# Expert units of one head by 128 tokens in place of four heads by 32 tokens

## The chip, the cores and the metric

The kernel runs on one core of one Trainium2 chip. The metric is the device time of one execution in microseconds (us). The kernel before took 1830.41 us (median of three runs, 1829.29 to 1832.8). All arrays are float32.

## What is computed

Two blocks follow one another on 256 tokens of width 1024. The first (four mixers and a dense MLP) is untouched by the change. The second has 16 more tokens in front ("meta"), and two layers, each of which ends in PEER, a lookup of experts:

```python
q = einsum('btd,dq->btq', hx, w_query)            # 8 heads x 2 halves x 128
s = einsum('bthpc,hpnc->bthpn', q, sub_keys)      # 128 scores in each half
top_s, top_i = top_k(s, 16)
cand = top_s[..., 0, :, None] + top_s[..., 1, None, :]
best_s, best_pos = top_k(cand, 16)                # 16 experts per token and head
gate = softmax(best_s)
act = gelu(einsum('btd,bthkd->bthk', hx, u[expert]))
y = einsum('bthk,bthkd->btd', gate * act, v[expert])
```

So each of 256 tokens takes 8 x 16 = 128 pairs of rows u and v in each of two layers. A pair stands as 2048 numbers (8 KB) in one table in HBM. Between the two PEER layers stands one attention layer (products with w_kv, w_q, w_o, a loop over eight pairs of heads, then the query product of the second PEER).

## The kernel before, in words

The PEER work of both layers is one long pipeline of 512 *slots*. A slot is one gather of 128 rows of the table (1 MB, one row for each partition). 16 slots make a *unit* and 32 units follow one another: 8 for each of layer 0 tile 0, layer 0 tile 1, layer 1 tile 0, layer 1 tile 1, a tile being 128 tokens. The text counts in steps x of four slots: step x holds slots 4x to 4x+3 and unit x//4.

Before the change a unit is (layer, tile, g, half): the 32 tokens of group g, with four heads side by side in the four quarters of the partitions. Two units (half 0 and 1) finish a group.

A slot passes through these places:
- GpSimd issues the gather (peer_gpsimd, L634) into one of eight buffers (RING = 8), once the slot eight before it has been used up (v_used).
- VectorE multiplies the u half of the row by the token's own row and sums it (dots_of, L675). The tokens' rows stand in PSUM banks 2 and 3 (rows_x); unit_rows (L647) puts them there anew for every group, after the last dot of the group before. dots_of waits for it (rows_ready).
- ScalarE makes a 128x32 matrix: gelu(dot) times a selection matrix (L706), then times the gate (L710). The selection matrix sel32 has a one where partition p belongs to token p mod 32.
- TensorE multiplies this matrix by the v half of the row, in two halves of 512 columns (slot_value, L662). The output has 32 partitions. Even slots write partitions 0 to 63 of the bank, odd slots 64 to 127, so that the four quarters of the array are used in turn; two banks alternate from group to group.
- After a group VectorE adds four pieces of 32x512 to the residual h (add_group, L722).

In each step TensorE executes, in the written order (peer_tensor, L775): late_queries_pe (steps 0 to 15: L384 scores, L366 transposes of the queries, L349 the query product of a later unit), then for each of the four slots pieces of the attention (attend_pe) and the slot's own product. ATTEND = (34, 66) is the step at which the attention of tile 0 and of tile 1 begins; from there count steps i. Products with weights (product, L824; L828 for the meta tokens, tile 0 only) stand in i = 2, 3 (query), 4, 5 (key), 6, 7 (value), and later for w_o and the second query product: four in a step, two before its first slot and two before its second. The loop over the pairs of heads starts at i = 9 (tile 0) or 8 (tile 1). The weights come through six buffers of 512 KB from SP's queue. VectorE's and ScalarE's orders are written out by hand in the same steps. The routing of units (top-16 searches) is spread over the steps by the tables EARLY and LATE.

At the end (s = 31) zero_products keeps TensorE busy between slots, the last group is added, and each group of 32 rows is stored on its own (L1660).

## Time and profile before

| | us |
|---|---|
| median of three runs | 1830.41 |
| lowest, highest | 1829.29, 1832.8 |
| span of the profiled execution, first to last instruction | 1826.5 |
| TensorE busy | 1366.8 |
| VectorE busy | 1169.7 |
| ScalarE busy | 597.3 |
| GpSimd busy | 551.0 |

The time of a run contains some us before the first and after the last instruction: 1830.4 less 1826.5 is 3.9 us. The PEER pipeline begins at about 388 us with the first gather and ends with the span. "Busy" of TensorE counts matmuls that overlap once. "PEclk" is the share of the full clock (2.4 GHz) that TensorE was granted: 1.0 is 2.4 GHz, 0.5 is 1.2 GHz, a value between is a mean over both.

### The profile page before, as it was taken

What the parts mean: (1) busy time and instruction counts of PE and PEld (TensorE: products, weight loads), DVE (VectorE), ACT (ScalarE), POOL (GpSimd) and SP (SyncE); (2) the same over time, 40 slices, a digit from 0 to 9 for tenths busy, and PEclk for the clock granted to TensorE, in tenths of its full rate; (3) what the DMA queues carried; (4) which work ended last, traced back from release to release, by engine and by line L of the source; (5) the groups of instructions that cost most, each with busy time, mean ns of one, the idle gap of its engine ahead of it and who ended that gap; (6) DMA issues with size and microseconds to landing.
All of it is one profiled execution on the core that took longest, in us unless ns stands there. A gap on an engine that the chain in (4) does not pass through costs nothing.

```text
span 1826.5 us, 21618 instructions
## 1 busy us (share of the span) xinstructions
PE 1366.8 (75%) x7080; PEld 550.5 (30%) x7080; DVE 1169.7 (64%) x2705; ACT 597.3 (33%) x1530; POOL 551.0 (30%) x633
## 2 busy tenths in 40 slices
PE   8999999988874545698678865776787765655566
PEld 7856666653430010122122221221232210101011
DVE  5831334277776777656786647767877577677764
ACT  2421011124342323433443323433443333333332
POOL 2001232023332333322433224322342333333331
PEclk9999999999996676799777878897898977666677
DMA  9048697559999999999999999999999999999997
GB/s 358 5 176 345 204 373 263 230 211 419 420 420 419 417 415 417 420 417 409 417 392 418 416 418 406 419 417 416 384 410 418 420 421 421 421 422 418 418 421 292
DMA packets 118194, 681.29 MB, mean 373 GB/s; under 512 B 11790, under 2 KB 13970, under 8 KB 50114
## 3 DMA queue, kind: packets, MB, share of 16 engines
q0 software_dynamic: 78336, 553.68, 73.6%
q1 hardware_dynamic: 39745, 126.23, 18.0%
q8 instruction: 56, 0.92, 0.2%
q14 instruction: 57, 0.46, 0.1%
HBM read 678.30 MB, written 1.05 MB: 372 GB/s over the span
## 4 chain that ended last, share of the span: by engine, by line
DMA 37%; PE 29%; DVE 13%; ACT 4%; issue 3%; DVEq 3%; POOL 2%; ACTq 1%; POOLq 0%
DMA big<-in_peer_uv,expert 33%; PE ps L662 7%; DVE big L675 6%; PE ps L1900 6%; PE ps L1889 6%; PE ps L824 5%; DMA normed<-in_peer_uv,expert 5%; DVEq L528 2%; POOL big L634 2%; PE ps L647 2%; DVE residual L722 1%; ACT placed L706 1%; ACT L706 1%; ACT placed L710 1%; ACT L683 1%
## 5 line engine op out<-in xcount | busy, mean ns | idle before, releaser
L662 PE MATMUL ps<-big,placed 128*32 128x512 f32 x1992 | 596.1, 795 | 393.9 <-ACT placed L710 391.8
L675 DVE CUSTOM_DVE_ANT_0 big<-big,ps 128x1024 f32<-128x1024 f32 x498 | 595.7, 1219 | 340.4 <-DMA big<-in_peer_uv,expert 322.9
L634 POOL DMA_INDIRECT big<-in_peer_uv,expert x498 | 473.8, 951 | 1016.7 <-PE ps L662 855.9
L706 ACT ACTIVATE placed<-sel,dots 128x32 f32<-128x32 f32 x512 | 163.5, 319 | 797.2 <-DVE dots L675 789.6
L662 PEld LDWEIGHTS ps<-big,placed 128*32 128x32 f32 x1992 | 80.8, 122 | 820.5 <-ACT placed L710 734.7
L824 PE MATMUL ps<-big 128*128 128x512 f32 x384 | 187.2, 624 | 2.5 <-DVE big L1129 1.4
L710 ACT ACTIVATE placed<-placed,gate 128x32 f32<-128x32 f32 x512 | 164.6, 321 | 35.4 <-issue 0.3
L1900 PE MATMUL ps<-big,sc 128*128 128x512 f32 x256 | 115.5, 595 | 0.0
L1889 PE MATMUL ps<-ua,big 128*128 128x256 f32 (+1 forms) x512 | 110.4, 370 | 2.9 <-PEq L75 2.9
L824 PEld LDWEIGHTS ps<-big 128*128 128x128 f32 x384 | 69.8, 196 | 116.6 <-issue 108.7
L1889 PEld LDWEIGHTS ps<-ua,big 128*128 128x128 f32 x512 | 94.1, 194 | 27.8 <-issue 17.7
L1725 ACT ACTIVATE sc<-ps 128x256 f32<-128x256 f32 (+1 forms) x32 | 11.8, 370 | 173.2 <-PE ps L1889 173.2
L1517 PE MATMUL ps<-sc,big 128*128 128x256 f32 x288 | 63.6, 379 | 1.9 <-DMA big<-in_w_in 1.6
L349 PE MATMUL ps<-big 128*32 128x256 f32 x1024 | 61.5, 394 | 3.6 <-DVE big L278 3.6
L1900 PEld LDWEIGHTS ps<-big,sc 128*128 128x128 f32 x256 | 48.0, 190 | 49.5 <-issue 48.1
L1517 PEld LDWEIGHTS ps<-sc,big 128*128 128x128 f32 x288 | 54.0, 189 | 11.0 <-DVE sc L1367 2.1
L611 POOL DMA_INDIRECT big<-in_peer_uv,expert x32 | 38.9, 1216 | 60.4 <-DVE expert L572 26.6
L706 ACT ACT_TABLE_LOAD x40 | 51.3, 1283 | 1.1 <-issue 0.5
L722 DVE TENSOR_TENSOR residual<-residual,ps 32x512 f32<-32x512 f32 x64 | 43.7, 684 | 2.4 <-PE ps L662 0.5
L647 PE MATMUL ps<-ident,big 128*32 128x128 f32 x960 | 43.6, 326 | 0.4 <-DVE dots L675 0.4
L675 DVE DVE_READ_ACCUMULATOR2_ANT dots<- 128x1 f32 x512 | 42.2, 82 | 0.0
L647 PEld LDWEIGHTS ps<-ident,big 128*32 128x32 f32 x960 | 36.1, 130 | 18.1 <-issue 10.3
(371 smaller groups left out, 1280.2 us busy)
## 6 DMA issues: line engine op xcount, KB each, us to landing
big<-in_mlp_w SPq DMA_DIRECT2D x16, 2048.0 KB, 15.9
big<-in_peer_wq SPq DMA_DIRECT2D x2, 8192.0 KB, 26.9
big<-in_w_kv SPq DMA_DIRECT2D x32, 512.0 KB, 14.2
big<-in_peer_wq SPq DMA_DIRECT2D x32, 512.0 KB, 13.2
big<-in_w_in SPq DMA_DIRECT2D x5, 2048.0 KB, 17.8
big<-in_peer_uv,expert POOLq DMA_INDIRECT x530, 15.0
big<-in_w_q SPq DMA_DIRECT2D x16, 512.0 KB, 14.0
big<-in_w_o SPq DMA_DIRECT2D x16, 512.0 KB, 10.3
```

What stands on the lines that cost most here:

```text
L349: last = nc.tensor.matmul(bank(4 + u % 2)[TOK * j:TOK * (j + 1), 0:256], hnt[:, k, at:at + TOK], wq_peer[:, k, cols:cols + 256], start=(k ...
L634: nc.gpsimd.indirect_dma_start(out=pair_row(n), out_offset=None, in_=rows, in_offset=bass.IndirectOffsetOnAxis(ap=expert[:, n // TOPK % DE ...
L647: last = nc.tensor.matmul(to[TOK * j:TOK * (j + 1), :], hnt[:, k, at:at + TOK], ident[:], start=True, stop=True)
L662: last = nc.tensor.matmul(acc[r:r + TOK, :], placed[:, n % RING, :], pair_row(n)[:, D + BANK * half:D + BANK * (half + 1)], start=(opens a ...
L675: nc.vector.tensor_tensor_reduce(out=row, in0=row, in1=rows_x, scale=1.0, scalar=0.0, op0=ALU.mult, op1=ALU.add, accum_out=dots[:, u % 2, ...
L706: a.activation(to, sel32[:], ACT.Gelu, scale=dots[:, u % 2, k:k + 1])
L710: a.activation(to, to, ACT.Copy, scale=gate[:, u % DEEP, k:k + 1]).then_inc(S(f"weights_ready{UNITS[u][0]}"), 1)
L722: last = v.tensor_tensor(to, to, bank(group % 2)[r:r + TOK, :], ALU.add)
L824: last = m.matmul(bank(b + half), src, w[:, BANK * half:BANK * (half + 1)], start=(k == 0), stop=(k == KD - 1))
L1517: last = m.matmul(bank(b)[:, T * c:T * (c + 1)], win[chunk][:, k, P * (at + c):P * (at + c + 1)], ht[:, k, :], start=(k == 0), stop=(k == ...
L1889: last = m.matmul(bank(4 + q % UP_BANKS)[:, first:T], w1b[c % 2][:, k, P * (q % FT):P * (q % FT + 1)], h2t[:, k, first:T], start=(k == 0), ...
L1900: last = m.matmul(bank(2 * t + half), act2[:, q % FT, P * t:P * (t + 1)], w2b[c % 2][:, q % FT, BANK * half:BANK * (half + 1)], start=(q = ...
```

## The change

A unit becomes (layer, tile, head): all 128 tokens of a tile and one head, one token for each partition.
- The matrix of a slot becomes 128x128 with the weights on the diagonal (gelu times the identity), and slot_value multiplies it over the whole width of the array. All 128 slots of a tile add up in banks 0 and 1.
- The four adds per group become two adds of 128x512 per tile (add_tile). They stand after the second dot of the next tile; the first product of the next tile waits for both.
- unit_rows runs once per tile and transposes eight 128x128 blocks.
- The query product, the scores and the second PEER's scores become 128 wide.
- The output is stored in halves of 512 columns for each tile.
- The matrix select, its four copies on GpSimd, and sel32 go.

```diff
-        placed = sb("placed", [P, RING, 32])
-        sel32 = sb("sel32", [P, 32])
+        placed = sb("placed", [P, RING, P])
@@ tile_units
-            return [(layer, t, g, half) for g in range(QUADS) for half in range(2)]
+            return [(layer, t, head) for head in range(PH)]
@@ queries_pe
-                for j in range(QUADS):
-                    cols = D * half + 256 * j
-                    last = nc.tensor.matmul(bank(4 + u % 2)[TOK * j:TOK * (j + 1), 0:256], hnt[:, k, at:at + TOK],
-                                            wq_peer[:, k, cols:cols + 256], start=(k == 0), stop=(k == KD - 1))
+                last = nc.tensor.matmul(bank(4 + u % 2)[:, 0:256], hnt[:, k, at:at + P],
+                                        wq_peer[:, k, 256 * head:256 * (head + 1)], start=(k == 0), stop=(k == KD - 1))
@@ scores0_pe
-            for j in range(QUADS):
-                for p in range(2):
-                    last = nc.tensor.matmul(bank(7)[TOK * j:TOK * (j + 1), P * p:P * (p + 1)],
-                                            q_cols[u % 2][:, P * p + TOK * j:P * p + TOK * (j + 1)],
-                                            keys_t0[:, 2 * (QUADS * half + j) + p, :], start=True, stop=True)
+            for p in range(2):
+                last = nc.tensor.matmul(bank(7)[:, P * p:P * (p + 1)], q_cols[u % 2][:, P * p:P * (p + 1)],
+                                        keys_t0[:, 2 * head + p, :], start=True, stop=True)
@@ unit_rows
-            slots_done(pe, "dots_done", TOPK * u)
+            if u:
+                slots_done(pe, "dots_done", TOPK * u)
             for k in range(KD):
-                to = bank(2 + k // 4)[:, P * (k % 4):P * (k % 4 + 1)]
-                for j in range(QUADS):
-                    last = nc.tensor.matmul(to[TOK * j:TOK * (j + 1), :], hnt[:, k, at:at + TOK], ident[:],
-                                            start=True, stop=True)
+                last = nc.tensor.transpose(bank(2 + k // 4)[:, P * (k % 4):P * (k % 4 + 1)], hnt[:, k, at:at + P], ident[:])
@@ slot_value
-            if k == 0 and opens and group >= 2:
-                pe.wait_ge(S("tile_out"), group - 1)
+            if first and u:
+                sums_out(pe, u // PH)
             slots_done(pe, "weights_ready", n + 1)
             for half in range(2):
-                r = 2 * TOK * (k % 2) + TOK * half
-                last = nc.tensor.matmul(acc[r:r + TOK, :], placed[:, n % RING, :],
-                                        pair_row(n)[:, D + BANK * half:D + BANK * (half + 1)],
-                                        start=(opens and k < 2), stop=(closes and k >= TOPK - 2))
+                last = nc.tensor.matmul(bank(half), placed[:, n % RING, :],
+                                        pair_row(n)[:, D + BANK * half:D + BANK * (half + 1)], start=first, stop=final)
@@ slot_weight
-            a.activation(to, sel32[:], ACT.Gelu, scale=dots[:, u % 2, k:k + 1])
+            a.activation(to, ident[:], ACT.Gelu, scale=dots[:, u % 2, k:k + 1])
@@ add_group becomes add_tile
-            for par in range(2):
-                slots_done(dve, "v_used", TOPK * (u + 1) - 1 + par)
-                for half in range(2):
-                    r = 2 * TOK * par + TOK * half
-                    to = h[TOK * g:TOK * (g + 1), t, BANK * half:BANK * (half + 1)]
-                    last = v.tensor_tensor(to, to, bank(group % 2)[r:r + TOK, :], ALU.add)
-                dve.drain()
-            last.then_inc(S("tile_out"), 1)
+            slots_done(dve, "v_used", TOPK * (u + 1))
+            for half in range(2):
+                to = h[:, t, BANK * half:BANK * (half + 1)]
+                step(dve, nc.vector.tensor_tensor(to, to, bank(half), ALU.add), "tile_out")
@@ peer_vector
-                    ahead = j == 0 and s > 0 and opens_group(s)
+                    ahead = j == 0 and s > 0 and opens_tile(s)
                     if ahead:
                         routes_at(dve, s, j)
-                    dots_of(dve, s, range(4 * j, 4 * j + 4))
-                    if j == 1 and s >= 1 and closes_group(s - 1):
-                        add_group(dve, s - 1)
-                    if not ahead:
+                        dots_of(dve, s, range(0, 2))
+                        add_tile(dve, s - 1)
+                        dots_of(dve, s, range(2, 4))
+                    else:
+                        dots_of(dve, s, range(4 * j, 4 * j + 4))
                         routes_at(dve, s, j)
@@ attend_pe (scores of the second PEER)
-                for g in range(QUADS):
+                for j in range(QUADS):
                     for p in range(2):
-                        for j in range(QUADS):
-                            hp = 2 * (QUADS * half + j) + p
-                            last = m.matmul(bank(6 + g // 2)[TOK * j:TOK * (j + 1), 256 * (g % 2) + P * p:256 * (g % 2) + P * (p + 1)],
-                                            qt1[:, hp, TOK * g:TOK * (g + 1)], keys_t1[:, hp, :], start=True, stop=True)
+                        hp = 2 * (QUADS * half + j) + p
+                        at = 256 * (j % 2) + P * p
+                        last = m.matmul(bank(6 + j // 2)[:, at:at + P], qt1[:, hp, :], keys_t1[:, hp, :], start=True, stop=True)
@@ the stores
-                    for g in range(QUADS):
-                        r = slice(TOK * g, TOK * (g + 1))
-                        sp.wait_ge(S("tile_out"), QUADS * (NT + t) + g + 1)
-                        sp.dma_start(out_v[r, t, :], h[r, t, :]).then_inc(S("out_stored"), 16)
+                    for half in range(2):
+                        cols = slice(BANK * half, BANK * (half + 1))
+                        sp.wait_ge(S("tile_out"), 2 * (NT + t) + half + 1)
+                        sp.dma_start(out_v[:, t, cols], h[:, t, cols]).then_inc(S("out_stored"), 16)
```

## Rows read from the trace of the kernel before

**Rows 1.** The page, part 2: the span in 40 slices of 45.7 us

```profile
DMA  9048697559999999999999999999999999999997
GB/s 358 5 176 345 204 373 263 230 211 419 420 420 419 417 415 417 420 417 409 417 392 418 416 418 406 419 417 416 384 410 418 420 421 421 421 422 418 418 421 292
```

**Rows 2.** Windows: us, busy of PE, PEld, DVE, ACT, POOL, PEclk, DMA share, GB/s

```profile
399.00:539.00 140.00, 117.74 (x1414) 52.84 (x1408) 111.18 (x289) 56.06 (x166) 51.71 (x55) 0.94 1.01 420
774.00:869.00 95.00, 84.25 (x339) 26.76 (x341) 55.58 (x122) 32.17 (x74) 22.47 (x24) 0.95 1.01 414
1510.00:1800.00 290.00, 171.32 (x652) 28.23 (x652) 204.17 (x469) 93.29 (x256) 107.80 (x115) 0.68 1.01 420
```

**Rows 3.** Windows: two stretches at borders of groups, same columns

```profile
927.00:944.00 17.00, 15.76 (x134) 6.46 (x134) 13.14 (x27) 7.90 (x27) 7.64 (x8) 0.91 0.93 338
1312.00:1332.00 20.00, 19.10 (x142) 8.43 (x140) 14.78 (x27) 9.22 (x27) 8.19 (x8) 0.82 0.87 324
```

**Rows 4.** Timeline, VectorE at the border before unit 20: start, us, what, [idle before]

```profile
1320.62 1.22 DVE L675 CUSTOM_DVE_ANT_0 big<-big,ps 128x1024 f32<-128x1024 f32 x1 [4.67 <-PE ps L647]
```

**Rows 5.** Groups with forms: busy, mean ns of one, idle before

```profile
L722 DVE TENSOR_TENSOR residual<-residual,ps 32x512 f32<-32x512 f32 x64 | 43.7, 684 | 2.4 <-PE ps L662 0.5
L706 ACT ACTIVATE placed<-sel,dots 128x32 f32<-128x32 f32 x512 | 163.5, 319 | 797.2 <-DVE dots L675 789.6 <-PE ps L662 6.8
L1730 ACT ACTIVATE sc<-sc 128x256 f32<-128x256 f32 x32 | 13.3, 416 | 2.6
```

**Rows 6.** Timeline, TensorE, a query product and the slots behind it

```profile
449.15 3.66 PE L349 MATMUL ps<-big 128*32 128x256 f32 x64
452.63 1.04 PE L662 MATMUL ps<-big,placed 128*32 128x512 f32 x8
```

**Rows 7.** Timeline, TensorE, around the head of the pipeline

```profile
383.18 3.72 PE L1993 MATMUL ps<-big 128*128 128x256 f32 x16
398.69 6.52 PE L349 MATMUL ps<-big 128*32 128x256 f32 x64 [3.58 <-DVE big L278]
```

**Rows 8.** Timeline, TensorE, products and slots of the attention of tile 0

```profile
782.69 3.70 PE L824 MATMUL ps<-big 128*128 128x512 f32 x8
786.35 1.05 PE L662 MATMUL ps<-big,placed 128*32 128x512 f32 x4
787.33 3.70 PE L824 MATMUL ps<-big 128*128 128x512 f32 x8
...
831.66 3.26 PE L647 MATMUL ps<-ident,big 128*32 128x128 f32 x58
...
836.10 1.88 PE L824 MATMUL ps<-big 128*128 128x512 f32 x4
837.92 1.05 PE L828 MATMUL ps<-big 128*32 128x512 f32 x4
838.90 1.99 PE L824 MATMUL ps<-big 128*128 128x512 f32 x4
...
849.32 1.98 PE L824 MATMUL ps<-big 128*128 128x512 f32 x4
```

**Rows 9.** The chain that ended last, gathers in it: issue, us to landing

```profile
529.84 15.34 DMA big<-in_peer_uv,expert
868.76 12.60 DMA big<-in_peer_uv,expert
```

**Rows 10.** Gathers issued from 1312 to 1332 (tile big, GpSimd)

```profile
DMA to landing us min/median/max: 7.4/8.7/10.6
```

**Rows 11.** Timeline, the last slot and the end

```profile
1819.89 1.04 PE L261 MATMUL ps<-zeros 128*128 128x512 bf16 x4
...
1821.38 1.05 PE L662 MATMUL ps<-big,placed 128*32 128x512 f32 x4 [0.45 <-ACT placed L710]
1822.47 1.40 DVE L722 TENSOR_TENSOR residual<-residual,ps 32x512 f32<-32x512 f32 x2 [0.48 <-PE ps L662]
```

**Rows 12.** Timeline, TensorE waiting in the loop over pairs of heads

```profile
1338.05 0.28 PE L905 MATMUL ps<-ident,big 128*16 128x128 f32 x1 [2.82 <-DVE big L1206]
```

More of the change, by code:

```diff
@@ L376, in scores0_pe @@
         def scores0_pe(pe, u):
-            half = UNITS[u][3]
+            head = UNITS[u][2]
             pe.wait_ge(S("q_out"), u + 1)
@@ L407, in peer_head_pe @@
             pe.wait_ge(S("h1"), 4)
-            for half in range(2):
-                last = nc.tensor.matmul(bank(2 + half), select[:], ffn0_rows[:, BANK * half:BANK * (half + 1)],
-                                        start=True, stop=True)
-            last.then_inc(S("rows_ready"), 1)
+            unit_rows(pe, 0)
             query_columns_pe(pe, 1)
@@ L1692, in _ @@
                 step(pool, g.memset(half_col[:], 0.5), "masks_ready")
-                for j in range(QUADS):
-                    step(pool, g.tensor_copy(select[:, TOK * j:TOK * (j + 1)], ident[:, 0:TOK]), "masks_ready")
                 pool.wait_ge(S("meta_q_done"), 1)
```

60 lines of the change are left out of this document (25 added, 35 removed).

## The prediction

> **What bounds the kernel now.** I read the page's slices first: from slice 9 (411 us) to the end the DMA engines are busy for 9 tenths or more, and move 410 to 422 GB/s in nearly every slice [rows 1]. A gather is 128 x 8192 bytes = 1.049 MB, so at 420 GB/s a slot costs 2.50 us and a step of four slots 9.99 us, whoever works on it. Then the windows: in the plain stretch 1510 to 1800 TensorE is busy 171 of 290 us at a mean clock of 0.68, VectorE 204 of 290, ScalarE 93 of 290 [rows 2]. None of them sets the pace there. In the first steps (399 to 539) TensorE is busy 118 of 140, and in the products of the first attention (774 to 869) 84 of 95, both near full clock [rows 2]. So the change can gain only where the DMA engines have holes, and lose where a grown engine passes them. The holes: 338 GB/s over 17 us and 324 over 20 us [rows 3], that is 17 x (1 - 338/420) = 3.3 us and 20 x (1 - 324/420) = 4.6 us, and some 2 us in smaller ones. After the last gather comes a chain that nothing hides [rows 11].
>
> **The price of a wide slot.** Before, a slot is four matmuls of 128x512 on 32 columns of the array, two of them side by side: 1.05 us alone and 0.98 us from its start to the next product [rows 8]. When TensorE is behind, an even and an odd slot run together: two slots in 1.04 us [rows 6]. After, the four are 128 columns wide and follow one another. The same form stands in L824: eight took 3.70 us and four 1.98 [rows 8], so four more cost 1.72 us in a stream. In the plain stretches a slot has 2.50 us, so 1.72 fits. At 1.2 GHz it would be 3.4 us and over the pace (an estimate, twice 1.72), but the rows show that TensorE holds 0.94 and 0.95 where it is busy for 84 to 89% of the time and 0.68 where it is busy for 59% [rows 2]. At 3.4 us per slot TensorE would never be idle, busier than in any of these stretches, so I expect the full clock throughout. Then TensorE has 2.50 - 1.72 = 0.78 us to spare per slot, and the plain stretches (steps 14 to 33, 60 to 66, 95 to 125) cost nothing. The DMA engines are the cover; without it each slot would cost 0.7 us.
>
> **First steps (0 to 12), where queries run beside slots.** A step after is a query product of 16 matmuls 128x256, 3.72 us alone [rows 7] and some 3.45 in a stream (the tail of 0.26 that 1.98 and 1.72 show goes), two transposes and four score matmuls of 128x128 at a quarter of 0.43 us, 0.65 together [rows 8], and four slots, 6.88: 11.0 us against 9.99 of DMA. The query product itself hardly changes: before, 64 narrow matmuls took 3.66 [rows 6]. From the first query at 398.69, which runs at low clock (6.52 us, and as 16 wide ones about 6.7) [rows 7]: 398.7 + 6.7 + 12 x 3.45 + 13 x 6.88 + 7.4 for columns and scores = 543.6 us for the end of step 12. This frees the buffer of slot 59, whose gather was issued at 529.84 and landed 15.34 us later, at 545.2 [rows 9]. The ring gives part back, since fewer gathers stand in the queues: where the DMA engines ran short, a gather landed in 7.4 to 8.7 us [rows 10]. So it lands at 551 to 552.5: **+7 us** (bounds 0, if a part of the wait is hidden by weights loaded at that time, and 12, if gathers still take 13 us to land).
>
> **First attention, key and value products (steps 38 to 41).** Here TensorE also has the meta products L828, 64 rows wide at most, beside which the narrow slots run in the other quarters of the array: step 40 goes from 836.10 to 849.32, 13.2 us, of which four pairs of L824 and L828 are 4 x 2.9 = 11.6 [rows 8]. So a slot cost 0.41 us there and costs 1.72 after: 16 x 1.31 = 21 us more. The eight slots of the query steps grow by 0.55 each, 4.4. One unit_rows goes, 3.3 us [rows 8]. 84.3 + 21 + 4.4 - 3.3 = 106.4 us of work in a stretch of 95 [rows 2]: TensorE ends it 11 us late. The gather issued at 868.76 and landed at 881.4 [rows 9] is issued at 880 and lands at 887.5 to 889, 6 to 7.5 later; weights are asked for late too, which may starve the queues, or arrive in time, which fills them: **+6 us** (2 to 12).
>
> **Other products with weights.** A step has two product pairs of 3.66 us, each followed by a slot, and two more slots. Before 11.1 us, after 4 x 1.72 + 4 x 1.72 = 13.8, against 4 x (1.049 + 0.524) MB = 15.0 us of DMA. It fits, with little to spare: 0. The exception is w_o of tile 1 (steps 83, 84), which starts just behind the second hole with few gathers under way: **+2 us** (0 to 5).
> What the rows show of neighbours: a narrow slot starts 3.66 us after the start of eight wide matmuls, though eight times 0.43 is 3.44, and the next wide one 0.98 after it, though twice 0.43 is 0.86: 0.1 to 0.2 us go at each change between narrow and wide [rows 8]. By the Trainium skill (TensorEngine Tiling (Array Packing), Key Properties) "Mode switching requires drain", which the row bears out. After, slots and products are in one mode, and that is in the 0.55 above; without it a slot would grow by 0.74 and the sum by some 2 us. The same page (Theoretical Speedup) promises up to four times for outputs of 32, which speaks against the whole change; the rows give it two slots in 1.04 us where TensorE was behind, and that is what the first steps and steps 38 to 41 lose.
>
> **Loops over pairs of heads.** The rest of a step there is scores, transposes and sums of 2.7 us (tile 0) or 3.5 (tile 1), an estimate from the matmuls of L895 to L922 at 0.43 us for 512 columns [rows 8] and a drain at each change of width, and TensorE waits at its start for VectorE (2.82 us in one) [rows 12]. With 6.88: 9.6 and 10.4 us, against 9.99. VectorE is relieved: 64 adds of 0.684 us become 8 of about 0.69, 43.7 less 5.5 = 38 us [rows 5], and rows_x is renewed 3 times in place of 15. At the border before unit 20 it stood 4.67 us [rows 4]. These waits close: -3.3 us at the most from the first hole and -4.6 from the second. I take -2.5 and -1, because TensorE is over the pace in the second loop: **-3.5 us** (-8 to +6).
>
> **Tile borders.** One pair of banks for all: the first product of a tile waits for both adds, 1.4 us, which wait for the last product; queued behind are TensorE's slots and then GpSimd's gathers. Three times, in stretches with 0.78 us per slot to spare: 0 (0 to 3).
>
> **ScalarE.** 128 columns in place of 32: between 0.319 and 0.416 us, the row of 256 columns [rows 5]; I take 0.40. 1024 x 0.08 = 82 us more, beside a third of load: 0, and 0.16 in the end chain. GpSimd's four copies and the select products stand off the path: 0.
>
> **The end.** Between the last seven slots stand four zero products each, 1.04 us alone [rows 11] and 0.86 in a stream (0.18 of drain goes, as above): 1.72 + 0.86 = 2.58 against a pace of 2.50, 0.6 late at the last. The last slot takes 1.98 in place of 1.05, ScalarE 0.16 more. The two adds stay 1.4 us [rows 11], the last store has 256 KB in place of 128, 0.3 more at 420 GB/s: **+2 us** (1 to 3).
>
> **Sum.** 7 + 6 + 2 - 3.5 + 2 = 13.5. On the profiled execution: 1826.5 + 13.5 = 1840; the median of the runs lies 3.9 us above that span, so 1844 us, 0.7% slower.
>
> **Rivals.**
> - *The ring covers it, and the borders decide (faster).* Eight buffers hold 20 us of gathers, and if the lags of 14 and 11 us in the two TensorE stretches are taken up wholly there, only the holes count: -7.9 and -1 of the small ones, +2 at the end: 1830.4 - 7 = 1823.5 us. For it: at steps 38 to 41 TensorE already lagged, and the window still shows 414 GB/s [rows 2]. Against: a gather cannot land faster than 7.4 us [rows 10]. It decides if the lag at the end of step 12 is under 6 us. Chance 0.17.
> - *Half is covered (no change).* The two losses are 3 us each and the holes close by 5: 1830 to 1834. Chance 0.10.
> - *TensorE sets the pace in the loops too (much slower).* If half of the wait for VectorE at the head of a step (2.82 us) [rows 12] stays uncovered, a step costs 9.6 or 10.4 plus 1.4 us, 1.0 and 1.8 over the pace: 18 steps make +26, the gain of 3.5 falls away too, and VectorE's relief gives some 5 back: 1844 + 25 = 1869. Chance 0.10.
> - *The clock stays at its mean of 0.68 to 0.8.* A slot would be 2.2 to 2.5 us: the pace itself, and the product steps would take 17 and more: over 1900. Against it is every dense row. Chance 0.03.
>
> **Numbers.** My forecast has 0.60: 1844, by its own bounds 1834 to 1858. With the rivals the range is 1824 to 1860. A measurement of this kernel tells 0.2% (3.7 us) from no change; faster 0.17, same 0.11, slower 0.72.
>
> **What would show it.** PEclk near 1.0 through the pipeline, TensorE over 95% busy in 399 to 545 with under 400 GB/s there, and again in 800 to 885; L662 in stream at 1.72 us per slot; no wait of VectorE for L647 at 930 and 1320, and 400 GB/s or more there. The plain stretches must stay at 420. If the first 150 us of the pipeline keep 420 GB/s, my largest term is wrong; if the loops fall under 400, the third rival holds.

## The result, and the profile after

The changed kernel takes 1849.28 us (median of 4 runs, 1848.58 to 1851.0), the kernel before 1830.8 beside it (4 runs, 1829.29 to 1832.8): 1.0104 times, 95% interval 1.009 to 1.0118, or 18.5 us more. The forecast was 1844, 0.7% slower.

| | before | after |
|---|---|---|
| median, us | 1830.8 | 1849.28 |
| span of the profiled execution | 1826.5 | 1849.0 |
| TensorE busy | 1366.8 | 1661.6 |
| VectorE busy | 1169.7 | 1132.8 |
| ScalarE busy | 597.3 | 676.6 |
| GpSimd busy | 551.0 | 550.4 |

The profiled execution of the changed kernel had 1851.0 us with a span of 1849.0, so 2.0 us lie around the span. By that the profiled execution of before (span 1826.5) was 2.3 us faster than the median of 1830.8 and that of after 1.7 us slower than its own: of the 22.5 us between the two traces about 4 are the spread between executions.

The page of the changed kernel: part 1, then TensorE, clock and DMA in 40 slices, then the chain that ended last, by engine and by line.

```profile
PE 1661.6 (90%) x4996; PEld 833.2 (45%) x4996; DVE 1132.8 (61%) x2648; ACT 676.6 (37%) x1530; POOL 550.4 (30%) x629
PE   9999999989997777899999997999999988777788
PEclk9999999989998998899999998999999999999999
GB/s 356 3 180 335 220 376 252 223 222 389 386 389 410 421 421 422 418 413 320 380 421 420 418 417 388 413 418 418 418 399 418 419 421 412 422 421 422 417 413 306
PE 55%; DMA 22%; DVE 7%; ACT 5%; issue 2%; DVEq 2%; ACTq 1%; POOL 0%; POOLq 0%
PE ps L648 27%; DMA big<-in_peer_uv,expert 20%; PE ps L804 8%; PE ps L1875 6%; PE ps L1864 6%; DVE big L660 3%; PE ps L346 3%; DMA normed<-in_peer_uv,expert 2%; DVEq L520 1%; ACT L691 1%; ACT placed L691 1%; ACT placed L695 1%; PE ps L808 1%; ACT L668 1%; ACTq L694 1%
```

Two places show in the GB/s (slices are counted from 0): 386 to 389 in slices 9 to 11, where [rows 1] has 419 and 420, and 320 and 380 in slices 18 and 19, where it has 409 and 417. In the chain TensorE's slot product (L648) is now the first entry with 27%; before (L662) it had 7%, and the gathers stood first.

Windows of the changed kernel, in us from the start of the span. Columns: length, busy of PE, PEld, DVE, ACT and POOL, PEclk, DMA share, GB/s. The first and the last have the times of [rows 2]. The second is the attention's products where they now lie. The third and the fifth have the times of [rows 3], but work stands 20 to 23 us later in this kernel, so they show the loops over pairs of heads ahead of the two borders; the borders themselves are the fourth and the sixth.

```profile
399.00:539.00 140.00, 138.97 (x471) 86.25 (x472) 104.56 (x275) 59.85 (x153) 46.51 (x49) 0.98 0.99 391
787.00:895.00 108.00, 103.93 (x273) 38.65 (x273) 55.66 (x131) 34.79 (x71) 22.67 (x24) 1.00 0.95 362
927.00:944.00 17.00, 15.30 (x51) 6.71 (x50) 14.73 (x35) 6.93 (x17) 5.71 (x6) 1.00 1.01 422
949.00:966.00 17.00, 17.00 (x59) 7.75 (x58) 12.47 (x24) 8.98 (x25) 6.37 (x7) 1.00 1.01 420
1312.00:1332.00 20.00, 20.00 (x76) 9.51 (x75) 17.42 (x39) 9.63 (x25) 7.92 (x8) 1.00 1.02 422
1332.00:1352.00 20.00, 18.61 (x66) 8.30 (x64) 17.57 (x35) 12.44 (x29) 6.57 (x7) 1.00 0.98 381
1510.00:1800.00 290.00, 225.25 (x464) 84.75 (x463) 202.21 (x481) 114.49 (x262) 108.06 (x115) 0.95 1.01 418
```

In the first 140 us of the pipeline TensorE is busy throughout, and the DMA engines move 391 GB/s in place of 420. In the attention's products they move 362 over 108 us. Of the two holes of [rows 3] the first is closed (420, before 338), the second only in part (381, before 324). The plain stretch has 418 (420 before), though TensorE works 225 us there in place of 171.

Where the 22.5 us arise is best read from one event in each step: the end of the last dot of the step (the READ_ACCUMULATOR rows of L660 after, L675 before). The table gives how much later than in the trace of before it is, in us. The table has the runs of the next section too, so that each can be read against the first line.

| step (time before) | 12 (526.5) | 15 (557.6) | 36 (780.8) | 45 (902.4) | 48 (936.5) | 51 (963.3) | 81 (1332.3) | 84 (1364.1) | 127 (1820.5) | end (1826.5) |
|---|---|---|---|---|---|---|---|---|---|---|
| changed kernel | 8.7 | 9.1 | 9.0 | 23.0 | 19.7 | 22.6 | 20.0 | 22.4 | 20.9 | 22.5 |
| e1_narrow_slots | 0.3 | -0.5 | 0.2 | 0.2 | -3.1 | -0.2 | -3.7 | 1.1 | -2.6 | -2.6 |
| e2_one_quarter | 11.7 | 13.8 | 14.0 | 28.4 | 24.4 | 27.2 | 24.3 | 25.7 | 25.6 | 28.8 |
| e7_before_serial | 12.6 | 17.4 | 15.9 | 29.0 | 29.4 | 30.6 | 25.5 | 26.4 | 28.2 | 32.7 |
| e4_blocks | -0.6 | -1.4 | -0.7 | -0.6 | -4.1 | -1.1 | -4.3 | 0.2 | -3.7 | -1.8 |
| e5_blocks_tile0 | 0.6 | 0.6 | 0.1 | 10.9 | 7.3 | 10.7 | 7.7 | 8.6 | 9.0 | 10.6 |
| e6_blocks_tile1 | 8.1 | 9.0 | 9.9 | 10.0 | 6.6 | 9.5 | 7.2 | 7.7 | 8.2 | 9.8 |
| e7_no_meta | 9.0 | 9.5 | 8.9 | 9.3 | 6.0 | 8.9 | 5.8 | 6.3 | 7.0 | 8.7 |
| e8_narrow_activations | 6.9 | 8.4 | 7.9 | 19.1 | 16.5 | 19.4 | 14.9 | 15.7 | 15.7 | 17.3 |
| e11_half_queries | -1.0 | -1.4 | -0.9 | 12.1 | 8.7 | 11.7 | 9.0 | 9.7 | 10.0 | 11.6 |
| e10_blocks_layer0 | -1.3 | -1.4 | -1.3 | -1.3 | -4.7 | -1.8 | -3.7 | -2.9 | -2.6 | -1.0 |

So the changed kernel loses 9.1 us up to step 15, nothing to step 36, 14.0 in the steps 36 to 45, gains about 2 up to step 127, and loses 1.6 at the end.

What TensorE does in the first steps, in its timeline: start, duration, line, operation, shapes.

```profile
467.84 0.61 PE L380 MATMUL ps<-gain_rows,ua 128*128 128x128 f32 x4
468.29 0.38 PE L363 MATMUL ps<-ident,ua 128*128 128x128 f32 x2
468.51 3.62 PE L346 MATMUL ps<-big 128*128 128x256 f32 x16
471.96 7.03 PE L648 MATMUL ps<-big,placed 128*128 128x512 f32 x16
478.83 0.61 PE L380 MATMUL ps<-gain_rows,ua 128*128 128x128 f32 x4
...
544.74 0.61 PE L380 MATMUL ps<-gain_rows,ua 128*128 128x128 f32 x4
```

There is no idle time in it. From one L380 to the next is a step, 10.99 us: 0.67 for scores and transposes, 3.45 for the query product, 6.87 for four slots of 1.72.

### The profile page after: what moved, and what is told of

Its sections match the earlier page's. It is cut to its first block, busy times and chain, and to the rows that moved or that the text cites. A ratio compares the mean times of both kernels' runs of the same rounds, so it can differ in the third digit from the quotient of the medians.

```text
span 1849.0 us, 17342 instructions
## 1 busy us (share of the span) xinstructions
PE 1661.6 (90%) x4996; PEld 833.2 (45%) x4996; DVE 1132.8 (61%) x2648; ACT 676.6 (37%) x1530; POOL 550.4 (30%) x629
## 4 chain that ended last, share of the span: by engine, by line
PE 55%; DMA 22%; DVE 7%; ACT 5%; issue 2%; DVEq 2%; ACTq 1%; POOL 0%; POOLq 0%
PE ps L648 27%; DMA big<-in_peer_uv,expert 20%; PE ps L804 8%; PE ps L1875 6%; PE ps L1864 6%; DVE big L660 3%; PE ps L346 3%; DMA normed<-in_peer_uv,expert 2%; DVEq L520 1%; ACT L691 1%; ACT placed L691 1%; ACT placed L695 1%; PE ps L808 1%; ACT L668 1%; ACTq L694 1%
## 5 line engine op out<-in xcount | busy, mean ns | idle before, releaser
L648 PE MATMUL ps<-big,placed 128*128 128x512 f32 x1992 | 949.8, 622 | 166.1 <-ACT placed L695 152.7
L660 DVE CUSTOM_DVE_ANT_0 big<-big,ps 128x1024 f32<-128x1024 f32 x498 | 598.2, 1220 | 351.2 <-DMA big<-in_peer_uv,expert 341.9
L648 PEld LDWEIGHTS ps<-big,placed 128*128 128x128 f32 x1992 | 374.7, 196 | 690.2 <-issue 384.9
L691 ACT ACTIVATE placed<-ident,dots 128x128 f32<-128x128 f32 x512 | 203.5, 397 | 581.7 <-DVE dots L660 574.1
L695 ACT ACTIVATE placed<-placed,gate 128x128 f32<-128x128 f32 x512 | 205.6, 402 | 35.4 <-issue 0.3
L804 PE MATMUL ps<-big 128*128 128x512 f32 x384 | 175.9, 594 | 0.0
L804 PEld LDWEIGHTS ps<-big 128*128 128x128 f32 x384 | 71.7, 190 | 89.2 <-issue 89.2
L346 PE MATMUL ps<-big 128*128 128x256 f32 x256 | 60.9, 393 | 3.0 <-DVE big L277 3.0
L346 PEld LDWEIGHTS ps<-big 128*128 128x128 f32 x256 | 49.5, 198 | 10.3 <-DVE big L277 3.4
L660 DVE DVE_READ_ACCUMULATOR2_ANT dots<- 128x1 f32 x512 | 42.3, 83 | 0.0
## 6 DMA issues: line engine op xcount, KB each, us to landing
big<-in_peer_wq SPq DMA_DIRECT2D x32, 512.0 KB, 10.8
```

The costliest lines, as they stand in the source:

```text
L346: last = nc.tensor.matmul(bank(4 + u % 2)[:, 0:256], hnt[:, k, at:at + P], wq_peer[:, k, 256 * head:256 * (head + 1)], start=(k == 0), sto ...
L648: last = nc.tensor.matmul(bank(half), placed[:, n % RING, :], pair_row(n)[:, D + BANK * half:D + BANK * (half + 1)], start=first, stop=final)
L660: nc.vector.tensor_tensor_reduce(out=row, in0=row, in1=rows_x, scale=1.0, scalar=0.0, op0=ALU.mult, op1=ALU.add, accum_out=dots[:, u % 2, ...
L691: a.activation(to, ident[:], ACT.Gelu, scale=dots[:, u % 2, k:k + 1])
L695: a.activation(to, to, ACT.Copy, scale=gate[:, u % DEEP, k:k + 1]).then_inc(S(f"weights_ready{UNITS[u][0]}"), 1)
L804: last = m.matmul(bank(b + half), src, w[:, BANK * half:BANK * (half + 1)], start=(k == 0), stop=(k == KD - 1))
```

## The experiments

**Is it the slot product at all?** The main theory T: TensorE loses time because the products of a slot follow one another (1.72 us) where before they ran side by side, in the two stretches in which TensorE has other products. The rival R: one of the other edits (the order of units, the wide query products, the one pair of accumulators, ScalarE's wider activations). In the changed kernel, only the slot product is put back on quarters:

```diff
-                last = nc.tensor.matmul(bank(half), placed[:, n % RING, :],
-                                        pair_row(n)[:, D + BANK * half:D + BANK * (half + 1)], start=first, stop=final)
+                r = 2 * TOK * (k % 2) + TOK * half
+                last = nc.tensor.matmul(bank(0)[r:r + TOK, :], placed[:, n % RING, 0:TOK],
+                                        pair_row(n)[:, D + BANK * half:D + BANK * (half + 1)],
+                                        start=(opens_tile(u) and k < 2), stop=(closes_tile(u) and k >= TOPK - 2))
```

> The changed kernel, but slot_value is again two products with a 32-column weight in four different quarters of TensorE's rows (two for the even, two for the odd slot), as in the kernel before; units, gathers, ScalarE's 128-column weights, query products and the sum at the end of a tile stay changed. It leaves out three of the four blocks of 32 tokens of every expert sum. Theory T (the loss is the time of a wide slot, 1.72 us against 1.04 us or less, where TensorE is behind): after the 12 first steps the delay against the kernel before is about +1 to +3 in place of +9, the first attention adds less than 4 in place of 14, the total is 1825 to 1833 us (0.998 +- 0.003 of before). Rival R (the loss is the new order of units, the other query and unit products, or ScalarE's wider activations, which all stay here): the total stays at 1845 to 1850 us.

Measured: 1825.78 us against 1828.4 of before beside it, 0.9983 (0.9973 to 0.9993). The whole loss is gone, and what is left of the change is worth some 3 us. R falls.

**Is it the width of the weight, or that the products don't run side by side?** The same kernel with a weight as narrow, but both products in the first quarter:

```diff
-                last = nc.tensor.matmul(bank(half), placed[:, n % RING, :],
+                last = nc.tensor.matmul(bank(half)[0:TOK, :], placed[:, n % RING, 0:TOK],
+                                        pair_row(n)[:, D + BANK * half:D + BANK * (half + 1)], start=first, stop=final)
```

> As e1_narrow_slots, but both products of every slot go to the same quarter, so that they run one after the other; the weight is as narrow as there. It leaves out three of the four blocks of 32 tokens of every expert sum. Theory T (what counts is that the products of a slot no longer run side by side, not the width of their weight): as slow as the changed kernel, 1845 to 1852 us, a slot in a stream 1.72 us. A rival within T (the 128-column weight load itself costs time): between e1_narrow_slots and the changed kernel, a slot in a stream under 1.6 us. Rival R: the same as e1_narrow_slots.

Measured: 1856.0 us, 1.0151 (1.0135 to 1.0168). So it is the lost overlap, not the width of the weight. The run is even 7 us slower than the changed kernel (9 by the ratios), which I had not expected. Its timeline:

```profile
470.33 0.38 PE L363 MATMUL ps<-ident,ua 128*128 128x128 f32 x2
470.55 3.62 PE L346 MATMUL ps<-big 128*128 128x256 f32 x16
474.10 7.05 PE L648 MATMUL ps<-big,placed 128*32 128x512 f32 x16
481.08 0.71 PE L380 MATMUL ps<-gain_rows,ua 128*128 128x128 f32 x4
481.63 0.38 PE L363 MATMUL ps<-ident,ua 128*128 128x128 f32 x2
```

Four slots take 7.05 us here and 7.03 with the wide weight. But a step is 481.63 - 470.33 = 11.30 us in place of 10.99: 0.1 us goes from the wide query product to the narrow slot (3.55 between their starts in place of 3.45), 0.1 on the way back, and 0.1 more before the transposes (0.55 in place of 0.45). Fourteen steps of 0.31 are 4.3 us, and the table shows 13.8 - 9.1 = 4.7 more at step 15.

**The same in the kernel before.** Here the old units stay, and only the slots lose their overlap:

```diff
-                r = 2 * TOK * (k % 2) + TOK * half
+                r = 0
-                                        start=(opens and k < 2), stop=(closes and k >= TOPK - 2))
+                                        start=(opens and k == 0 and half == 0), stop=(closes and k == TOPK - 1 and half == 1))
@@ add_group
-                slots_done(dve, "v_used", TOPK * (u + 1) - 1 + par)
+                slots_done(dve, "v_used", TOPK * (u + 1))
```

> The kernel before with one edit: all products of slot_value go to the first quarter of the rows of their bank, so that none runs beside another; its units of four heads by 32 tokens, its query products in four quarters, its unit rows of 64 products and its sums per group stay. It computes the expert sums wrongly (both halves of the columns are added in the same place). Theory T: +8 to +10 in the first steps and +12 to +16 in the first attention, as the change has, and on top of it some microseconds at the borders of the groups, since the 64 products for the unit's rows and the wait for both last slots stay: 1848 to 1856 us. Rival R (reordering, query products, ScalarE's width): near the kernel before, 1830 to 1836 us.

Measured: 1862.08 us, 1.0186 (1.0169 to 1.0203). The mechanism is that of T, the size was 6 us beyond my range. What I had left out is seen in the timeline: the 64 products of unit_rows stand among the slots in the first steps too, where TensorE has nothing to spare (490.06, 490.91).

```profile
485.76 4.88 PE L662 MATMUL ps<-big,placed 128*32 128x512 f32 x11
490.06 0.42 PE L647 MATMUL ps<-ident,big 128*32 128x128 f32 x6
490.48 0.59 PE L662 MATMUL ps<-big,placed 128*32 128x512 f32 x1
490.91 1.91 PE L647 MATMUL ps<-ident,big 128*32 128x128 f32 x58
```

Between this kernel and the changed one lie 13 us (15 by the ratios), but the changed one has no changes between narrow and wide at its slots. The fair partner is e2_one_quarter, which has the new units and the same narrow slots in a row: 1856.0 against 1862.08, so the rest of the change is worth 6 us once TensorE is the engine that is behind.

**Can the overlap be had with the new units?** The diagonal weight has four blocks of 32 x 32 that are not zero. They can be multiplied alone, each with its own 32 rows of the pair, and the second half one quarter further, so that eight blocks have a place of their own (the new slot_value and the second half of the sum; the 32-column weights of ScalarE are left out here):

```diff
@@ slot_value
+            for i in range(QUADS):
+                for half in range(2):
+                    r, c = TOK * i, TOK * ((i + half) % QUADS)
+                    last = nc.tensor.matmul(bank(half)[c:c + TOK, :], placed[r:r + TOK, n % RING, :],
+                                            pair_row(n)[r:r + TOK, D + BANK * half:D + BANK * (half + 1)],
+                                            start=first, stop=final)
@@ add_tile
...
+            for i in range(QUADS):
+                r, c = TOK * i, TOK * ((i + 1) % QUADS)
+                to = h[r:r + TOK, t, BANK:2 * BANK]
+                last = nc.vector.tensor_tensor(to, to, bank(1)[c:c + TOK, :], ALU.add)
```

> The changed kernel, but the diagonal weight of a slot is kept as its four 32 x 32 blocks (ScalarE writes 32 columns as in the kernel before) and slot_value is eight products of a 32 x 32 block with 32 rows of the gathered pair, each with its own quarter of rows and of columns; the second half's sums stand one quarter further and are added in four pieces. It computes all of the reference. If blocks in different rows and columns run side by side as the quarters of the kernel before do: a slot in a stream takes 0.9 to 1.2 us, and the total is 1822 to 1832 us, the loss of the changed kernel gone and its savings at the borders left. If products that share only the columns or only the rows wait for each other: a slot takes 1.72 us or more and the total is 1845 us or more; fully one after the other it would be 8 x 0.86 = 6.9 us a slot and the kernel twice as slow as TensorE's 512 slots of 6.9 us allow, over 3500 us.

Measured: 1827.56 us against 1828.4, 0.9998 (0.9989 to 1.0008). In its timeline a slot (16 instructions now) takes 1.09 us alone, and three take 2.80:

```profile
479.41 3.62 PE L347 MATMUL ps<-big 128*128 128x256 f32 x16
482.96 2.80 PE L651 MATMUL ps<-big,placed 32*32 32x512 f32 x48
486.01 1.09 PE L651 MATMUL ps<-big,placed 32*32 32x512 f32 x16 [0.25 <-ACT placed L699]
```

So the loss is gone here with all of the work done. But the gain at the borders doesn't show in the median: the sum of a tile takes 3.5 us at the end in place of 1.4 (in the table -3.7 at step 127 becomes -1.8 at the end), and the rest is within the spread.

**How much does each stretch cost, and does the first make the second dearer?** Blocks in one tile of layer 0 and wide slots elsewhere (`u // PH in (0,)`, then `(1,)`; the blocks are cut from the same 128-column weight).

> The changed kernel with its slots of the first tile of layer 0 (steps 0 to 31) as eight products of 32 x 32 blocks, cut out of the same 128-column weight, and wide slots in all other steps. It computes all of the reference. Theory T with inheritance (the first attention cost 14 in place of my 6 because TensorE came into it late): the first steps' +9 goes, and the first attention adds 5 to 9 in place of 14, total 1829 to 1835 us. Theory T without inheritance (the backlog made in the attention's own steps is what counts): the first steps' +9 goes and the attention still adds 13 to 16, total 1838 to 1842 us. Rival R (not the slots): 1845 us or more.

> The changed kernel with its slots of the second tile of layer 0 (steps 32 to 63, with the whole first attention) as eight products of 32 x 32 blocks, and wide slots in all other steps. It computes all of the reference. Theory T: +9 in the first steps as in the changed kernel, then 0 to 3 in the first attention in place of 14, the borders of the steps 48 and 80 earlier by 3 for a while, total 1833 to 1838 us. Rival R: 1845 us or more.

Measured: blocks in tile 0 (steps 0 to 31) 1838.85 us, 1.0054 (1.0037 to 1.0071); blocks in tile 1 (steps 32 to 63) 1837.43 us, 1.0044 (1.0027 to 1.0061). With the first, the first steps cost nothing and the attention 10.8; with the second, the first steps cost 9.0 and the attention 0.1. The total of the first is as "without inheritance" said, but the attention's term (10.8) lies between the two answers (5 to 9, and 13 to 16). The second came as theory T said. The windows, first those of e5, then those of e6:

```profile
399.00:539.00 140.00, 120.35 (x1194) 64.70 (x1194) 109.63 (x290) 64.95 (x166) 52.98 (x57) 0.95 1.01 420
787.00:895.00 108.00, 103.93 (x279) 39.00 (x278) 54.48 (x127) 41.79 (x85) 25.58 (x28) 1.00 0.96 371
```

```profile
399.00:539.00 140.00, 137.58 (x471) 85.22 (x472) 105.97 (x278) 60.10 (x153) 47.10 (x50) 0.99 0.99 394
787.00:895.00 108.00, 96.18 (x680) 27.51 (x672) 62.87 (x145) 44.19 (x91) 30.39 (x31) 0.93 1.01 415
```

Each stretch has its DMA rate back where its slots are blocks: 420 in the first steps of e5 (371 in its attention), 415 in the attention of e6 (394 in its first steps).

**Is it TensorE's sum of work in the attention?** The products of the meta tokens are cut:

```diff
-                for half in range(2):
+                if k in (0, KD - 1):
+                    for half in range(2):
```

> The changed kernel without 24 of its 32 products for the 16 meta tokens' keys and values in the attention of tile 0 (6 of the 8 chunks, keys and values each; the meta tokens' keys and values are summed from two chunks only). TensorE loses 48 instructions of about 0.4 us in steps 38 to 41 where run alone, so up to 10 us if they are on the path (two halves beside each other: 5 us). Theory T (TensorE's sum of work in steps 36 to 42 is the path): the first attention adds 4 to 10 in place of 14, total 1839 to 1846 us. Rival (a wait of VectorE or of the gathers of one head is the path there): no change, 1847 to 1851 us.

Measured: 1837.6 us, 1.0047 (1.003 to 1.0063). The effect is larger than I had expected, in the direction of T: the attention adds 0.4 us in place of 14.0. I had taken the price of a meta product too low. In the changed kernel four L804 and four L808 take 816.04 to 821.73, 5.69 us for two chunks; without L808 two chunks take 3.44 (821.20 to 824.63 in this run). That is 1.13 us for each of the 12 left out, 13.5 us. TensorE's timeline of the changed kernel, two chunks:

```profile
816.04 1.88 PE L804 MATMUL ps<-big 128*128 128x512 f32 x4
817.85 1.05 PE L808 MATMUL ps<-big 128*32 128x512 f32 x4
818.84 1.98 PE L804 MATMUL ps<-big 128*128 128x512 f32 x4
820.75 1.05 PE L808 MATMUL ps<-big 128*32 128x512 f32 x4
821.73 1.98 PE L648 MATMUL ps<-big,placed 128*128 128x512 f32 x4
```

**Is it TensorE's sum of work in the first steps?** `for k in range(KD)` of queries_pe runs over every second chunk from unit 2 on.

> The changed kernel with only 4 of the 8 chunks in the query products of units 2 to 15, which leaves out half of the sum of each query of layer 0. TensorE's step falls from 11.0 us to about 9.3, under the 10.0 us that the DMA engines need for its four gathers. Theory T (the sum of TensorE's work per step is what the first steps lose): the +9 of the first steps goes to about +1 to +2, the attention still adds 12 to 15, total 1838 to 1843 us. Rival (another wait, such as the weight of a slot or the query columns, sets the 11.0 us): +5 or more stays in the first steps, 1845 us or more.

Measured: 1840.23 us, 1.0067 (1.0052 to 1.0083), as theory T said. At step 15 it stands at -1.4 in place of +9.1, and the attention adds 13.0. So in the first steps wide slots cost nothing once the step is under the pace of the DMA engines.

**Is it ScalarE?** The two activations of a slot on columns 0 to 31 only.

> The changed kernel with ScalarE's two activations per slot on 32 columns in place of 128; the other 96 columns of the weight are zeros, and the products stay 128 columns wide. It leaves out three of the four blocks of 32 tokens of every expert sum. Theory T: ScalarE's width costs nothing but the last slot's, about 0.2 us in all and at most 2 where TensorE waited for a weight: 1846 to 1849 us. Rival (ScalarE's 512 x 0.16 us longer activations are on the path): a slot's weight comes 0.16 us earlier each, 10 us or more in all, 1838 us or less.

Measured: 1847.52 us, 1.0101 (1.0084 to 1.0118). The two activations take 0.318 and 0.322 us in place of 0.397 and 0.402, 82 us less in sum, and the kernel is 1.8 us faster by the medians, inside the spread (the intervals of the two ratios overlap nearly wholly).

**A version that beats both?** Three more, with all of the work done: e4_blocks with the last tile's blocks kept in their own quarter, so that two additions suffice at the end (e9); the changed kernel with blocks in layer 0 and wide slots in layer 1 (e10); and e10 without the zero products between the last slots (e12).

```diff
@@ e9
+                    shift = half if u // PH < 3 else 0
+                    r, c = TOK * i, TOK * ((i + shift) % QUADS)
@@ e10
+            if u // PH in (0, 1):
@@ e12
-                        if s + 1 == units and j >= 2 and (j, q) != (3, 3):
-                            zero_products(pe, 4)
```

> The kernel of e4_blocks (32 x 32 blocks for every slot, 32-column activations), but in the last tile of layer 1 both halves keep their quarter, so that four blocks run beside each other in place of eight (a slot about 1.72 us) and the sum at the end is two additions of 128 rows in place of one and four of 32. It computes all of the reference. Theory: e4_blocks lost 2 us at the end (3.5 us of additions in place of 1.4) and nothing is lost in the last tile, where the DMA engines set the pace: the last 8 us shrink to about 6.5, total 1822 to 1829 us, 0.998 of before (0.997 to 0.999). Rival: blocks in one quarter wait for their start in the ring, the last tile becomes slower by 0.1 us per slot or more: 1830 us or more.

> The changed kernel with blocks of 32 x 32 in all slots of layer 0 (steps 0 to 63) and wide slots in all of layer 1 (steps 64 to 127, with the second attention); ScalarE writes 128 columns throughout. It computes all of the reference. Theory T (wide slots cost nothing where the DMA engines set the pace, and the two TensorE stretches are all of the loss): 1825 to 1830 us, the losses of e5 and e6 removed together. Rival (my second forecast term: TensorE sets the pace in the second attention, or at w_o of tile 1): 2 to 8 us more from step 66 on, 1830 to 1836 us.

> e10_blocks_layer0 without the four zero products that stand between the last seven slots of the kernel. It computes all of the reference. In the trace of e10 the last dot ends at 1817.97, its weight at about 1818.4, and the last slot starts at 1819.74, since each slot (1.72 us) and its zero products (0.86 us) take 2.58 us and more against a pace of 2.50. Theory: with wide slots alone TensorE keeps its clock (0.96 to 1.00 in the last slices) and the last slot starts about 0.2 us behind its weight: 1 us less than e10, 1824 to 1829 us, 0.999 of before. Rival: without the zero products the clock falls for the last slots, which then take up to 3.4 us each: the end 1 to 3 us later than in e10, 1828 to 1832 us.

Measured: e9 1828.57 us, 1.0003 (0.9994 to 1.0012); e10 1827.08 us, 0.9995 (0.9986 to 1.0004); e12 1827.85 us, 0.9993 (0.9984 to 1.0002). None can be told from the kernel before. e10 shows no cost of wide slots in the whole of layer 1, its attention too (from -1.8 at step 51 to -2.6 at step 127, and a median as that of e4_blocks); the rival with 2 to 8 us more there falls. e9 missed what it was built for, though its median lies inside the stated range: from its last dot to its end are 9.3 us (1817.7 to 1827.0; 6.0 in the kernel before), because a slot of four blocks beside four takes 1.94 us and the zero products 1.04, 2.84 us from slot to slot against 2.50. The end of e9, TensorE and VectorE:

```profile
1818.28 1.94 PE L652 MATMUL ps<-big,placed 32*32 32x512 f32 x16
1820.15 1.04 PE L261 MATMUL ps<-zeros 128*128 128x512 bf16 x4
1821.12 1.94 PE L652 MATMUL ps<-big,placed 32*32 32x512 f32 x16
1823.16 1.41 DVE L709 TENSOR_TENSOR residual<-residual,ps 128x512 f32<-128x512 f32 x2 [5.39 <-PE ps L652]
```

In e12 the last slot starts 0.06 us after its weight and takes 1.98 us, and PEclk is 1.00 from 1800 to 1822, so the clock holds without the zero products. From the last dot to the end are 6.8 us in place of the 7.6 of e10, but the 1 us forecast doesn't show in the median:

```profile
1819.54 0.40 ACT L703 ACTIVATE placed<-placed,gate 128x128 f32<-128x128 f32 x1
1820.00 1.98 PE L656 MATMUL ps<-big,placed 128*128 128x512 f32 x4 [0.49 <-ACT placed L703]
```

## Why the prediction was right, and where its sizes were off

**The bound and the price of a slot: right.** The step that carried the forecast, that a slot costs 1.72 us and hurts only where TensorE has other products, is what the rows show. PEclk is 0.95 to 1.00 in the windows of the changed kernel; the plain stretch stays at 418 GB/s; TensorE is busy for 145 of the 146 us from 399 to 545 and for 82 of the 85 from 800 to 885, as foretold, with 392 and 361 GB/s. e11 and e7_no_meta take the two losses away by taking work of other products away, e5 and e6 by making the slots short.

**First steps: +7 forecast, 8.4 to 9.5 measured** (the four traces with wide slots and the 128-column product there). The work of a step was 11.0 by the forecast and is 10.99. The end of step 12, forecast 543.6, is 544.7 (the first query started 1.3 us later than I had taken). Two small steps failed. (The sum was loose in two more places: the 7.4 us for columns and scores would be 12 x 0.65 = 7.8, and a landing 7.4 to 8.7 us after 543.6 is 5.8 to 7.1 us late, of which I took the upper end.) The gather of slot 59 was issued at 545.18 and its dot began at 554.61 (VectorE's timeline):

```profile
554.61 1.22 DVE L660 CUSTOM_DVE_ANT_0 big<-big,ps 128x1024 f32<-128x1024 f32 x1 [1.24 <-DMA big<-in_peer_uv,expert]
```

so it took 9.4 us (VectorE was idle for 1.24 before, waiting for it), not the 7.4 to 8.7 that I had read from a stretch with far fewer gathers under way [rows 10]. And there are 14 query products in the steps (units 2 to 15 in steps 0 to 13), not 13: one more step over the pace (step 13, with its query product at 545.40 and its end at 555.72). It shows as only 0.4 us between steps 12 and 15 of the table; why so little I did not follow up.

**First attention: +6 forecast, 14.0 measured in the changed kernel; 10.8, 11.2 and 13.0 in e5, e8 and e11.** This is the term that was mis-sized. Its sum of work came out right, with one loose reading: a pair of L824 and L828 takes 2.8 us in [rows 8] (836.10 to 838.90), not 2.9, which would have made the 21 us some 1.5 less. From the first product of step 36 to the issue of the gather that step 41 frees, the forecast has 11 us more, and the traces have 895.22 - 787.24 = 108.0 against 868.76 - 772.11 = 96.7, 11.3 more. Wrong was the start. I let the stretch begin where it began before. It began at 787.24 in place of 772.11, 15.1 us late, while the dots were 9.0 late: 6 us of new backlog that TensorE had on entry. TensorE's timeline ahead of it shows why:

```profile
772.41 6.46 PE L648 MATMUL ps<-big,placed 128*128 128x512 f32 x8 [4.35 <-ACT placed L695]
778.71 1.04 PE L825 MATMUL ps<-ident,big 128*128 128x128 f32 x8
779.68 0.66 PE L831 MATMUL ps<-ident,big 16*128 16x16 f32 x8
780.27 7.13 PE L648 MATMUL ps<-big,placed 128*128 128x512 f32 x16
787.24 3.60 PE L804 MATMUL ps<-big 128*128 128x512 f32 x8
```

TensorE waits 4.35 us for a weight, and behind the wait the granted clock is low (PEclk 0.57 from 772 to 779; 8 matmuls in 6.46 us in place of 3.4). Six slots in all stand before the products, these two and four more that are cleared one by one at 1.72 us. In the kernel before, much the same wait (4.25 us) was followed by slots that ran side by side, 12 matmuls in 2.52 us, and the products began 9.3 us after it, here 14.8:

```profile
762.80 2.52 PE L662 MATMUL ps<-big,placed 128*32 128x512 f32 x8 [4.25 <-ACT placed L710]
...
767.40 2.52 PE L662 MATMUL ps<-big,placed 128*32 128x512 f32 x12
...
772.11 3.70 PE L824 MATMUL ps<-big 128*128 128x512 f32 x8
```

A narrow slot cleared a backlog at twice the pace of the DMA engines and more (about 1 us against 2.50); a wide one at 1.72 gains 0.8 us per slot. So "the plain stretches cost nothing" holds for the DMA engines, but each wait of VectorE's in them reaches the dense stretch behind. What the ring gives back (the second of my sub-steps, 4 to 5 us) was about right: the gather issued at 895.22 landed 8.24 us later in place of 12.60 [rows 9]; in the chain of the changed kernel it stands as

```profile
895.22 8.24 DMA big<-in_peer_uv,expert
```

11.3 + 6 - 4.4 = 13 us, against 14.0 in the table. The entry backlog is made locally, not inherited from the first steps: in e5, without any delay before step 36, the products still begin 3.4 us late (775.54 in place of 772.11). There the wait ahead of the six slots was 3.29 us and the first eight matmuls took 3.70, and the term is 10.8; the 2.7 us less of backlog are most of the 3.2 less in the term. The other two traces with wide slots lie between: in e11 the eight take 6.01 us behind a wait of 4.35, the backlog on entry is 5.6 us (products at 776.84, dots 0.9 early) and the term 13.0; in e8 they take 5.40 behind 3.96, the backlog is 4.7 (784.68, dots 7.9 late) and the term 11.2. So backlog and term go together in four traces, and e11 has nearly all of it without any delay before step 36. What the low clock alone adds I read off, and did not test.

**Loops, borders of groups, w_o: -3.5 + 2 forecast, -2.1 measured** (23.0 at step 45, 20.9 at step 127). VectorE's wait for unit_rows [rows 4] is gone, and the steps 48 and 81 show it at once: 3.3 and about 3 us less delay. By the steps 51 and 84 most of it is given back. Here a step of the forecast failed, that the holes in the transfers are VectorE's waits and close with them. In e1_narrow_slots no dot waits for unit_rows either, and the DMA engines still run short at both borders, in the windows of [rows 3] with 338 and 324 before:

```profile
927.00:944.00 17.00, 14.84 (x72) 4.70 (x71) 12.66 (x26) 9.24 (x26) 8.60 (x10) 0.79 0.91 344
1312.00:1332.00 20.00, 19.48 (x104) 8.35 (x102) 18.12 (x33) 12.95 (x33) 9.92 (x10) 0.80 0.90 342
```

So the dots came earlier there and the transfers did not. In the changed kernel the second hole is still there in part (381), and the window from 1332 to 1400, with w_o in it, has 402 GB/s where the kernel before has 420. What makes the holes stays open. The loss at w_o of tile 1 (from step 81 to 84) is 2.4 us in the changed kernel, close to the 2 of the forecast. That wide slots cause it is not shown: it is 4.8 in e1_narrow_slots and 4.5 in e4_blocks, which have none, and 0.8 in e10, which has them there. What stays of the whole is 2 to 3 us, in e1_narrow_slots too (-2.6 at the end). The third rival (TensorE sets the pace in the loops) falls: the loops of tile 0 and tile 1 have 422 GB/s in the changed kernel (927 to 944, 1312 to 1332), and e10 has no loss in layer 1.

**Tile borders, ScalarE: nothing, as forecast** (e8). **The end: +2 forecast, +1.6 measured**: 6.0 us from the last dot before, 7.6 after. The last slot's product and the two additions, in the timeline after as [rows 11] before:

```profile
1843.22 1.88 PE L648 MATMUL ps<-big,placed 128*128 128x512 f32 x4
1845.14 1.41 DVE L703 TENSOR_TENSOR residual<-residual,ps 128x512 f32<-128x512 f32 x2 [3.71 <-PE ps L648]
```

**From the sum to the median.** 13.5 us forecast, 22.5 between the traces, 18.5 between the medians. I had put 3.9 us between the span and the median of 1830.41; 2.0 of it lies around the span and 1.9 was the chance of the profiled execution. Between the traces the forecast was 9 us short, between the medians 5; that the second is smaller is luck of the executions that were profiled. The first attention alone, 8 us short, is most of it.

## What to carry to other kernels

When an engine is off the critical path, ask how fast it clears a backlog, not only whether its mean load fits. Products that run side by side on quarters of the array are a reserve that no table of busy time shows: TensorE was 75% busy before, and the reserve (about 1.0 us per slot against 1.72) was needed in two stretches of some 150 and 108 us only, yet all of the loss came from there. And work that is taken away beside a bounding engine gives only what that engine cannot win back in the next steps: some 930 matmul instructions of unit_rows and 56 additions went, and about 3 us came of it.

## What the runs showed of the hardware

- Eight fp32 products of a 32 x 32 block with 512 columns, four rows of blocks writing into one PSUM bank at the same time, take 1.09 us alone and 0.93 in a row (48 in 2.80), where the same instructions one after another would need some 16 x 0.43 = 6.9 (an estimate, from the 0.43 us of a wide one with 512 columns). That four rows of blocks write at the same time is read from these times. Four beside one another (e9) take 1.94. The Trainium skill (TensorEngine Tiling (Array Packing), Restrictions and Gotchas) says "Different row tiles cannot access same PSUM bank simultaneously"; in e4_blocks they do, each in its own quarter of the partitions.
- Products in a row cost the same with a weight of 32 or 128 columns (four slots in 7.05 and 7.03 us, e2_one_quarter and the changed kernel). The change between the two shapes costs about 0.1 us each way.
- TensorE kept 0.95 of its clock while busy for 78% of a stretch (225 of 290 us), and 0.68 in the same stretch of the kernel before, busy for 59%. So the forecast of a full clock for the wide slot held, but for short stretches behind a wait: 0.57 from 772 to 779, behind 4.35 us without a matmul.
